# Starting products with three weight chunks at once, and copying a 128 MB table in 1 MB pieces beside the weight stream, in a two-block transformer kernel

## The chip, the cores and the metric

The kernel runs on one core of one Trainium2 chip. The metric is the device time of one execution in microseconds. Between runs of this kernel a difference of about 0.2% can be told from none.

## The reference, cut to what matters

Two transformer blocks are applied to 512 tokens of width 1024, all in float32. The first has a modulation (a product of a conditioning vector with a 1024 x 6144 matrix), RMS norms, neighbourhood attention, a gated recurrent mixer (HGRN2) and a feed-forward part (PEER) that gathers rows of two tables. The second block has two layers, each a mixer, a layer norm, a gated feed-forward part with a short convolution, and a second layer norm.

```python
h  = modulate(rms_norm(x, norm1), sh1, sc1) @ w_in      # q k v | hq zf zb i g; k v zf zb i of 256 context tokens too
x  = x + gt1 * (concat([na_x, hg_x]) @ w_out)
x  = x + gt2 * peer_ffn(modulate(rms_norm(x, norm2), sh2, sc2), peer_wq, peer_keys, peer_u, peer_v)
...                                                     # peer_ffn: for each token 128 rows of u and of v (16384 x 1024 each)
x  = rms_norm(x, norm_f)
for l in range(2):                                      # second block
    x = layer_norm(ALPHA * x + mixer(x), ln1_g[l], ln1_b[l])
    x = layer_norm(ALPHA * x + conv_ffn(x), ln2_g[l], ln2_b[l])
```

## The kernel before

All five engines run programs written out by hand, kept in step by semaphores; at 19 points (`barrier(eng, n)`) an engine drains itself (`eng.drain()`, line 161), counts up `phase` and waits until four engines have done so. With `passing` it counts up without waiting.

**Weights.** All weights come as one stream of chunks of 512 KB (128 partitions x 1024 numbers). `SECTIONS` gives their order: 16 chunks for the first part of the modulation (`mod1`), 4 each for q, k, v, hq, zf, zb, i, g, then `mod2` (24) and `mod3` (8), `out` (8), `wq` (16), and the second block's `rq`, `rk`, ..., `out_e`, `up0`, `down0`, `dq`, ..., `out_o`, `up1`, `down1`; `FIRST[name]` is a section's first chunk. SyncE (SP) loads chunk c into slot c % 4 of `RING` once chunk c - 4 has been used (line 366). VectorE splits each chunk of a product into a high part and a low part (`split_chunk`, lines 1289 and 1291). For most products three chunks are split ahead of need (`first_chunks`).

**Products.** One chunk gives 128 output features for all 512 tokens: for each of 8 input tiles k (128 features) `three_passes` issues high x high, high x low and low x high (lines 192 to 194), 24 matmuls of 512 columns in all. `tiles` runs the chunks of a section one after the other, with three PSUM banks in turn. After a norm, or where the mixer's output is new, the input tiles are themselves made one by one: VectorE scales a tile (line 1324), ScalarE applies gain and shift (973), VectorE splits it (1305, 1307) and counts up `x_split`. The first chunk of such a product waits for its tile before each three matmuls (`split(name, k)`). `follow` is the work that TensorE does for the next norm or, in `wq`, for the key scores behind each chunk. The `up` products are a loop of their own (`weights_up`) with four banks.

**The table.** The gathers of PEER read rows of one internal table `PEER_UV` (16384 x 2048) in which row n holds row n of u beside row n of v. The kernel makes it by copies from HBM to HBM: `copy_rows`, 32 copies of 1024 rows (4 MB) each, all issued by GpSimd (POOL): 9 before barrier 1, 15 between barriers 1 and 2 (from the ninth copy on each waits for the copy eight before it), and one at every fourth of the 32 attention tiles, between barriers 2 and 3. GpSimd waits for all of them before the first gather.

**Order of the work.** Norm of x and context; `mod1` on TensorE; splits of 8 x tiles and 8 context tiles; q, then barrier 1 for all engines but TensorE, which only passes it; k to g; barrier 2; 32 attention tiles, in each of which GpSimd makes a bias tile (line 402); barrier 3; the recurrent mixer in two directions with the `mod2` and `mod3` chunks placed in it (`modulate`, line 550), six of them at the start of each direction; barrier 6; `out`, norm, `wq`, PEER, norm; second block.

Of the kernel before, what the change touches and what calls it, by code (L numbers as in the profile page):

```python
# [26 lines left out]
D = 1024  # L27
# [27 lines left out]
EXP_AT = [24, 88] + [SLOTS * j + 56 for j in range(1, TT - 1)]  # L55
COPY_ROWS = 1024
COPIES = 2 * NKEYS * NKEYS // COPY_ROWS
COPIES_AHEAD = 8

# [7 lines left out]
for _name, _n in SECTIONS:  # L67
    FIRST[_name] = NCHUNK
    NCHUNK += _n


# [27 lines left out]
def build(nc, t):  # L99
    ctx = ExitStack()  # L100
    place = {}
    with ctx:
# [219 lines left out]
        def after(eng, s, key, n, per):  # L322
# [12 lines left out]
        pk_s, pk_sc, pk_top, pk_exp, pk_idx = (sem(f"pk_{k}") for k in ("s", "sc", "top", "exp", "idx"))  # L335
        uv_copied = [sem(f"peer_uv_copied{j}") for j in range(COPIES_AHEAD)]
        row_landed = [sem(f"row_landed{j}") for j in range(NROW)]
# [10 lines left out]
                                          "sum", "root")}  # L348

        nc_block = ctx.enter_context(nc.Block())  # L350


        @nc_block.sync
        def _(sp):
            sp.dma_start(XL[:], t["xl"]).then_inc(s_in, 16)
            sp.dma_start(PAR[:], t["par"]).then_inc(s_in, 16)
            sp.dma_start(XC[:], t["xc"]).then_inc(s_in, 16)
            sp.dma_start(IDN[:], t["ident"]).then_inc(s_in, 16)
            sp.dma_start(ONES[:], t["ones"]).then_inc(s_in, 16)
            for j in range(NSLOT):  # L360
                sp.dma_start(RING[:, j, :], t["wstream"][j]).then_inc(w_landed[j], 16)
            with sp.Fori(1, NCHUNK // NSLOT) as g:
                for j in range(NSLOT):

                    sp.wait_ge(chunk_used, g * NSLOT + (j - NSLOT + 1))
                    sp.dma_start(RING[:, j, :], t["wstream"][g * NSLOT + j]).then_inc(w_landed[j], 16)
            sp.wait_ge(phase, 4 * 19)
            sp.dma_start(t["out"], XL[:]).then_inc(s_out, 16)
            sp.wait_ge(s_out, 16)
# [3 lines left out]
        def _(pool):  # L373
            steps = Steps(pool, pool_step)
            pool.dma_start(BT, t["na_bias"]).then_inc(s_bt, 16)
            copies = iter(range(COPIES))

            def copy_rows(n):

                for i in itertools.islice(copies, n):  # L380
                    rows, x = slice(COPY_ROWS * (i // 2), COPY_ROWS * (i // 2 + 1)), i % 2
                    if i >= COPIES_AHEAD:
                        pool.wait_ge(uv_copied[i % COPIES_AHEAD], 16 * (i // COPIES_AHEAD))
                    pool.dma_start(PEER_UV[rows, D * x:D * x + D], t[("peer_u", "peer_v")[x]][rows]
                                   ).then_inc(uv_copied[i % COPIES_AHEAD], 16)

            pool.wait_ge(s_in, 80)
            copy_rows(9)
            barrier(pool, 1)
            copy_rows(15)  # L390
            barrier(pool, 2)
# [3 lines left out]
            for i in range(NA_HEADS * NCB):  # L395
                h, b = divmod(i, NCB)
                off = QB * b - KC0[b]
                if i >= 3:
                    pool.wait_ge(na["s"], i - 2)
                if i % 4 == 0:  # L400
                    copy_rows(1)
                pool.tensor_tensor(NBM[i % 3].rearrange("p (k j) -> p k j", k=NA_KH), BT[:, h, :, QB - off:QB - off + KB],
                                   par("na_mask")[:, KB * b:KB * b + KB].unsqueeze(1).to_broadcast([P, NA_KH, KB]),
                                   ALU.add).then_inc(na["bias"], 1)
# [29 lines left out]
            barrier(pool, 7)  # L434
            for j in range(COPIES_AHEAD):
                pool.wait_ge(uv_copied[j], 16 * (COPIES // COPIES_AHEAD))
            pool.wait_ge(chunk_used, FIRST["wq"] + 16)
# [27 lines left out]
        def _(pe):  # L465
# [11 lines left out]
            def tiles(c, n, xs, name, to, free, base=0, xs2=None, to2=None, follow=None):  # L477

                for i in range(n):
                    pe.wait_ge(w_split, nth_split(c + i) + 1)  # L480
# [6 lines left out]
                    for k in range(KT):  # L487
                        if b == 0:
                            split(name, k)
                        mm = three_passes(to(b), parts(c + i, k), tile(xs, k), pe, k == 0, k == KT - 1)  # L490
# [351 lines left out]
            def ffn(l):  # L842

                u, c0 = up[l], FIRST[f"up{l}"]
                with pe.Fori(0, 2 * FT // BLK) as g:
                    for j in range(BLK):
                        weights_up(pe, u, c0, g, j)
                for j in range(2 * FT % BLK):
                    weights_up(pe, u, c0, 2 * FT // BLK, j)
                after(pe, u, "act", 4 + FT, FT)  # L850
# [20 lines left out]
            def weights_up(pe, u, c0, g, j):  # L871
                pe.wait_ge(w_split, g * BLK + (nth_split(c0 + j) + 1))
                pe.wait_ge(u["evac"], g * BLK + (2 * FT * u["use"] + j + 1))
                for k in range(KT):
                    if j == 0:
                        split(("x3", "x5")[u["use"]], k)
                    mm = three_passes(bank(j % 4), parts(c0 + j, k), tile(XFS, k), pe, k == 0, k == KT - 1)
# [63 lines left out]
            passing(pe, 17)  # L941

            tiles(FIRST["out_o"], KT, MIXS, "mix3", main, ln[2], follow=mean(ln[2]))
            variance(ln[2])
# [974 lines left out]
```

## Time and profile before

| | us |
|---|---|
| median of 3 runs (lowest, highest) | 3895.64 (3894.32, 3897.06) |
| the profiled execution, its own time | 3882.41 |
| its span | 3880.6 |
| TensorE busy, share of the span | 3198.9, 82% |
| VectorE busy, share of the span | 2138.6, 55% |

The span is the time from the first to the last instruction that the profiler saw; all times "at" some microsecond count from its start. The profiled execution was 0.34% faster than the median of the timed runs, so its rows are used for differences, and a difference is then taken off the median.

### The profile page before, as it was taken

How to read it: one execution, taken by the hardware profiler on the slowest of the kernel's cores; microseconds unless marked ns; L12 is line 12 of the kernel's file. 1: busy time of each engine (PE TensorE's matmuls, PEld its weight loads, DVE VectorE, ACT ScalarE, POOL GpSimd, SP SyncE). 2: the span in 40 equal slices, each digit the busy share in tenths (PEclk: the TensorE clock that was granted, in tenths of full speed). 3: DMA queues.
4: the chain of work that ended last, by engine and by line, in shares of the span. 5: the costliest groups of instructions: out<-in, count | busy, mean ns of one | idle time of the engine just before them, and what ended most of it. 6: DMA issues, size and time to landing. Idle time of an engine off the chain costs nothing. (4 is left out here: it accounts for less than half of the span.)

```text
span 3880.6 us, 34820 instructions
## 1 busy us (share of the span) xinstructions
PE 3198.9 (82%) x12170; PEld 2142.1 (55%) x12170; DVE 2138.6 (55%) x3672; ACT 890.6 (23%) x2174; POOL 691.3 (18%) x655
## 2 busy tenths in 40 slices
PE   6499888788777777777777789778999899779998
PEld 6388677666222222322222267366887686458876
DVE  2122368656776774685444462346774434767753
ACT  2011333122222222222222220151220102312201
POOL 0000234101444343443343320000000000000000
PEclk6699888899999999999999999579999998889999
DMA  9999852125999999999999822001332230013322
GB/s 356 298 337 350 266 180 82 60 66 196 421 421 422 417 417 421 416 410 421 418 419 422 373 84 87 0 1 60 98 97 87 86 99 28 1 49 98 97 87 71
DMA packets 152752, 845.71 MB, mean 218 GB/s; under 512 B 13793, under 2 KB 14049, under 8 KB 86049
## 3 DMA queue, kind: packets, MB, share of 16 engines
q0 software_dynamic: 107968, 678.73, 44.8%
q1 hardware_dynamic: 44640, 165.12, 13.5%
q8 instruction: 84, 1.38, 0.1%
q14 instruction: 60, 0.48, 0.0%
HBM read 841.70 MB, written 136.31 MB: 252 GB/s over the span
## 5 line engine op out<-in xcount | busy, mean ns | idle before, releaser
L721 PE MATMUL PS<-AR,HC 128*128 128x512 f32 x1536 | 726.7, 618 | 249.0 <-ACT HC L1138 247.4
L192 PE MATMUL PS<-AR_r,RHI 128*128 128x512 f32 x1888 | 767.9, 407 | 182.9 <-DVE AR_r L1307 94.3
L194 PE MATMUL PS<-AR_r,RING_r 128*128 128x512 f32 x1888 | 746.7, 396 | 0.0
L1492 DVE SCALAR_TENSOR_TENSOR AR<-AR 128x1024 f32<-128x1024 f32 x384 | 470.2, 1225 | 359.7 <-DMA AR<-peer_uv,XC 356.9
L721 PEld LDWEIGHTS PS<-AR,HC 128*128 128x128 f32 x1536 | 283.5, 194 | 691.3 <-ACT HC L1138 393.2
L193 PE MATMUL PS<-AR_r,RHI 128*128 128x512 f32 x1504 | 594.8, 395 | 0.0
L445 POOL DMA_INDIRECT AR<-peer_uv,XC x384 | 398.7, 1038 | 739.8 <-PE PS L721 545.0
L192 PEld LDWEIGHTS PS<-AR_r,RHI 128*128 128x128 f32 x1888 | 361.8, 192 | 292.8 <-issue 89.7
L1289 DVE CAST RHI<-RING 128x1024 fp32r<-128x1024 f32 x256 | 178.6, 698 | 582.7 <-DMA RING<-in_wstream 519.3
L194 PEld LDWEIGHTS PS<-AR_r,RING_r 128*128 128x128 f32 x1888 | 362.2, 192 | 77.4
L193 PEld LDWEIGHTS PS<-AR_r,RHI 128*128 128x128 f32 x1504 | 288.6, 192 | 62.6 <-issue 6.0
L1291 DVE TENSOR_TENSOR RING_r<-RING,RHI 128x1024 fp32r<-128x1024 f32 x256 | 315.8, 1234 | 8.8
L721 PE MATMUL PS<-RHI_f,HC 128*128 128x512 f32 x512 | 240.0, 612 | 83.8 <-ACT HC L1138 82.4
L1129 ACT ACTIVATE XC<-XC 128x2 f32<-128x2 f32 x256 | 52.0, 203 | 924.7 <-DVE AR L1492 924.5
L1492 DVE SCALAR_TENSOR_TENSOR AR<-RHI_f,AR 128x1024 f32<-128x1024 f32 x128 | 156.6, 1225 | 122.9 <-DMA RHI_f<-peer_uv,XC 122.6
L721 PEld LDWEIGHTS PS<-RHI_f,HC 128*128 128x128 f32 x512 | 93.3, 192 | 230.2 <-ACT HC L1138 133.1
L1138 ACT ACTIVATE HC<-IDN,HC 128x128 f32<-128x128 f32 x512 | 173.7, 386 | 0.0
L445 POOL DMA_INDIRECT RHI_f<-peer_uv,XC x128 | 132.3, 1033 | 190.6 <-PE PS L721 186.8
L193 PE MATMUL PS<-HL_r,RHI 128*128 128x512 f32 x384 | 153.1, 399 | 0.0
L550 PE MATMUL PS<-CS,RING 128*128 128x2 f32 x768 | 129.2, 304 | 15.8 <-POOLq L161 10.6
L459 POOL DMA_DIRECT2D AR<-in_strips x1 | 0.7, 664 | 775.6 <-DVEq L161 775.6
L550 PEld LDWEIGHTS PS<-CS,RING 128*128 128x128 f32 x768 | 129.5, 267 | 16.8 <-POOLq L161 10.8
(314 smaller groups left out, 3677.8 us busy)
## 6 DMA issues: line engine op xcount, KB each, us to landing
RING<-in_wstream SPq DMA_DIRECT2D x304, 512.0 KB, 3.6
peer_uv<-in_peer_u POOLq DMA_DIRECT2D x16, 4096.0 KB, 80.6
peer_uv<-in_peer_v POOLq DMA_DIRECT2D x16, 4096.0 KB, 83.5
AR<-peer_uv,XC POOLq DMA_INDIRECT x384, 13.6
XL<-in_xl SPq DMA_DIRECT2D x1, 2048.0 KB, 9.9
RHI_f<-peer_uv,XC POOLq DMA_INDIRECT x128, 13.6
AR<-in_strips POOLq DMA_DIRECT2D x1, 2048.0 KB, 10.3
out_x<-XL SPq DMA_DIRECT2D x1, 2048.0 KB, 6.3
```

Of the source, the lines that this page charges most:

```text
L192: pe.matmul(out, sh, mh, start=start, stop=False)
L193: pe.matmul(out, sh, ml, start=False, stop=False)
L194: return pe.matmul(out, sl, mh, start=False, stop=stop)
L445: pool.indirect_dma_start(ROWS_UV[n % NROW], None, PEER_UV, bass.IndirectOffsetOnAxis(ap=IDX[:, n:n + 1], axis=0)).then_inc(row_landed[n % ...
L459: pool.dma_start(STRIP, t["strips"]).then_inc(s_strip, 16)
L550: mm = pe.matmul(bank(7, 2 * i, 2), part(RING, c + i, P * k, P), CS[:, 2 * k:2 * k + 2], start=(k == 0), stop=(k == KT - 1))
L721: mm = pe.matmul(bank(2 * (tt % 2) + x), DIAG[:, n % NDIAG, :], ROWS_UV[n % NROW][:, D + 512 * x:D + 512 * x + 512], start=(j == 0), stop= ...
L1129: act.activation(GA[:, n:n + 2], RAW[:, n:n + 2], ACT.Gelu).then_inc(gelu, 1)
L1138: act.activation(DIAG[:, (n + x) % NDIAG, :], IDN[:], ACT.Copy, scale=WEIGHT[:, n + x:n + x + 1]).then_inc(diag_ready, 1)
L1289: dve.tensor_copy(hi, x).then_inc(w_high, 1)
L1291: dve.tensor_tensor(lo, x, hi.bitcast(F32), ALU.subtract).then_inc(w_split, 1)
L1492: dve.scalar_tensor_tensor(JUNK[n % 2], ROWS_UV[n % NROW][:, 0:D], 1.0, HT[:, n // SLOTS, :], ALU.mult, ALU.mult, accum_out=RAW[:, n:n + 1 ...
```

## The change

The copies become 128 of 256 rows (1 MB). 96 of them are issued by SP, in the same queue as the weights: one after each weight chunk from the first of q to the last of `wq`, and two after every fourth chunk of `mod2` and `mod3`. The other 32 are issued by GpSimd, one before each bias tile of the attention, with a semaphore of their own. No copy waits for another one. GpSimd issues none before barriers 1 and 2. SP's loop is written out for the chunks up to `wq`.

In `tiles`, a section that begins at bank 0 takes its first three chunks together: TensorE waits until the third is split, and then does nine matmuls per input tile, three for each chunk, into three banks. This is so for q, `out`, `wq`, `rq`, `out_e`, `dq` and `out_o`, and `ffn` does the same by hand for `up0` and `up1`. The chunk counts go up only in the last input tile, and `follow(0)` comes right behind. Before `out_o` TensorE also waits for three of the roots, since banks 0 to 2 hold their sums.

```diff
-COPY_ROWS = 1024
+COPY_ROWS = 256
 COPIES = 2 * NKEYS * NKEYS // COPY_ROWS
-COPIES_AHEAD = 8
+COPIES_AFTER, _n = {}, 0
+for _c in range(FIRST["q"], FIRST["rq"]):
+    _more = 2 if FIRST["mod2"] <= _c < FIRST["out"] and _c % 4 == 0 else 1
+    COPIES_AFTER[_c] = range(_n, _n + _more)
+    _n += _more
+assert _n + NA_HEADS * NCB == COPIES
...
+        def copy_rows(eng, i, done):
+
+            rows, x = slice(COPY_ROWS * (i // 2), COPY_ROWS * (i // 2 + 1)), i % 2
+            eng.dma_start(PEER_UV[rows, D * x:D * x + D], t[("peer_u", "peer_v")[x]][rows]).then_inc(done, 16)
...
-            for j in range(NSLOT):
-                sp.dma_start(RING[:, j, :], t["wstream"][j]).then_inc(w_landed[j], 16)
-            with sp.Fori(1, NCHUNK // NSLOT) as g:
+            for c in range(FIRST["rq"]):
+                if c >= NSLOT:
+                    sp.wait_ge(chunk_used, c - NSLOT + 1)
+                sp.dma_start(RING[:, c % NSLOT, :], t["wstream"][c]).then_inc(w_landed[c % NSLOT], 16)
+                for i in COPIES_AFTER.get(c, ()):
+                    copy_rows(sp, i, uv_copied)
+            with sp.Fori(FIRST["rq"] // NSLOT, NCHUNK // NSLOT) as g:
...
-            pool.wait_ge(s_in, 80)
-            copy_rows(9)
             barrier(pool, 1)
-            copy_rows(15)
             barrier(pool, 2)
...
-                if i % 4 == 0:
-                    copy_rows(1)
+                copy_rows(pool, COPIES - 1 - i, uv_copied_late)
...
-                for i in range(n):
+                together = 3 if base == 0 else 0
+                if together:
+                    pe.wait_ge(w_split, nth_split(c + together - 1) + 1)
+                for k in range(KT if together else 0):
+                    split(name, k)
+                    for i in range(together):
+                        mm = three_passes(to(i), parts(c + i, k), tile(xs, k), pe, k == 0, k == KT - 1)
+                        if k == KT - 1:
+                            mm.then_inc(chunk_used, 1)
+                if together and follow is not None:
+                    follow(0)
+                for i in range(together, n):
...
+                pe.wait_ge(w_split, nth_split(c0 + 2) + 1)
+                pe.wait_ge(u["evac"], 2 * FT * l + 3)
+                for k in range(KT):
+                    split(("x3", "x5")[l], k)
+                    for j in range(3):
+                        mm = three_passes(bank(j), parts(c0 + j, k), tile(XFS, k), pe, k == 0, k == KT - 1)
+                        if k == KT - 1:
+                            mm.then_inc(chunk_used, 1)
+                weights_up(pe, u, c0, 0, 3)
                 with pe.Fori(0, 2 * FT // BLK) as g:
-                    for j in range(BLK):
+                    for j in range(4, 4 + BLK):
                         weights_up(pe, u, c0, g, j)
...
+            pe.wait_ge(df["root"], 3)
             tiles(FIRST["out_o"], KT, MIXS, "mix3", main, ln[2], follow=mean(ln[2]))
```

## Rows read from the trace of the kernel before

**Rows 1.** The page: the span in 40 slices of 97 us, two of its rows.
```profile
PE   6499888788777777777777789778999899779998
...
GB/s 356 298 337 350 266 180 82 60 66 196 421 421 422 417 417 421 416 410 421 418 419 422 373 84 87 0 1 60 98 97 87 86 99 28 1 49 98 97 87 71
```

**Rows 2.** Timeline about barrier 1: start us, us, instruction, idle before and what ended it.
```profile
105.35 0.43 DVE L1307 TENSOR_TENSOR HC_r<-HC,XC_r 128x256 fp32r<-128x256 f32 x1
165.30 0.69 DVE L1289 CAST RHI<-RING 128x1024 fp32r<-128x1024 f32 x1 [59.53 <-POOLq L161]
...
111.97 0.39 PE L194 MATMUL PS<-AR_r,RING_r 128*128 128x512 f32 x1
167.31 0.80 PE L192 MATMUL PS<-AR_r,RHI 128*128 128x512 f32 x1 [54.95 <-DVE RING_r L1291]
```

**Rows 3.** Timeline of POOL, 30 to 520 us, the rows behind its two long drains.
```profile
165.86 0.75 POOL L384 DMA_DIRECT2D peer_uv<-in_peer_v  x1 [126.21 <-POOLq L161]
...
407.75 0.55 POOL L392 DMA_DIRECT2D XC<-in_level_masks  x1 [116.22 <-POOLq L161]
```

**Rows 4.** Timeline: the last instruction ahead of barrier 2; PE and SP behind barrier 3.
```profile
395.04 0.60 ACT L1044 ACTIVATE AR<-PS 128x512 f32<-128x512 f32 x1 [4.84 <-PE PS L194]
...
528.84 20.64 PE L550 MATMUL PS<-CS,RING 128*128 128x2 f32 x96 [10.55 <-POOLq L161]
532.60 25.67 SPq L366 DMA_DIRECT2D RING<-in_wstream  x7
```

**Rows 5.** Stages: window, length, busy us (instructions) of PE, PEld, DVE, ACT, POOL, PEclk, DMA share, GB/s.
```profile
17.00:165.00 148.00, 81.48 (x360) 72.15 (x360) 31.90 (x59) 18.45 (x23) 6.43 (x9) 0.62 0.99 332
408.00:529.00 121.00, 108.37 (x577) 78.16 (x577) 51.55 (x129) 42.03 (x97) 32.85 (x43) 0.89 0.98 287
528.80:751.50 222.70, 180.73 (x1288) 175.52 (x1288) 163.88 (x209) 66.26 (x67) 86.21 (x60) 0.81 0.26 76
```

**Rows 6.** DMA issues (KB each, median us to landing); then landing of the first four chunks alone.
```profile
RING<-in_wstream SPq DMA_DIRECT2D x304, 512.0 KB, 3.6
...
DMA to landing us min/median/max: 14.3/15.4/17.7
```

**Rows 7.** Timeline of `mod1`: the matmuls of its last 12 chunks.
```profile
44.41 41.12 PE L550 MATMUL PS<-CS,RING 128*128 128x2 f32 x192 [3.08 <-DMA RING<-in_wstream]
```

**Rows 8.** POOL in one attention tile with a copy, and in one without.
```profile
443.78 0.77 POOL L384 DMA_DIRECT2D peer_uv<-in_peer_v  x1 [2.63 <-PE PS L601]
...
449.85 0.73 POOL L402 TENSOR_TENSOR HC<-AR,PAR 128x256 f32<-128x256 f32 x1 [2.41 <-PE PS L601]
```

**Rows 9.** PE alone by window: first chunk of `wq`, its next two; first of `up0`, of `up1`; q's three.
```profile
822.30:833.50 11.20, 10.07 (x24) 0.72 0.00 0
833.50:844.40 10.90, 10.90 (x49) 1.00 0.31 96
2688.50:2699.80 11.30, 9.10 (x25) 0.84 0.00 0
3475.60:3486.80 11.20, 9.59 (x24) 0.77 0.00 0
93.10:112.20 19.10, 19.02 (x72) 0.87 1.02 318
```

**Rows 10.** Timeline: neighbouring matmuls at the low clock; roots, last tile and next sum of `out_o`.
```profile
168.33 0.63 PE L194 MATMUL PS<-AR_r,RING_r 128*128 128x512 f32 x1
168.76 0.63 PE L192 MATMUL PS<-AR_r,RHI 128*128 128x512 f32 x1
...
3367.16 4.74 ACT L960 ACTIVATE HL<-PS,PAR 128x512 f32<-128x512 f32 x8
...
3409.93 0.80 PE L192 MATMUL PS<-AR_r,RHI 128*128 128x512 f32 x1 [3.59 <-DVE AR_r L1307]
...
3424.39 1.02 PE L531 MATMUL PS<-XL,ONES 128*128 128x512 f32 x2
```

**Rows 11.** Drains of POOL: ns min/median/max, first and last start in us.
```profile
L161 POOLq DRAIN  x19: 34/53/126390, 38.9 to 3486.0; - x19
```

More of the change, by code:

```diff
@@ L11 @@
-import itertools
 from contextlib import ExitStack
@@ L335, in build @@
         pk_s, pk_sc, pk_top, pk_exp, pk_idx = (sem(f"pk_{k}") for k in ("s", "sc", "top", "exp", "idx"))
-        uv_copied = [sem(f"peer_uv_copied{j}") for j in range(COPIES_AHEAD)]
+        uv_copied, uv_copied_late = sem("peer_uv_copied"), sem("peer_uv_copied_late")
         row_landed = [sem(f"row_landed{j}") for j in range(NROW)]
@@ L375, in _ @@
             pool.dma_start(BT, t["na_bias"]).then_inc(s_bt, 16)
[L376 to L385, printed above, removed]
-            pool.wait_ge(s_in, 80)
-            copy_rows(9)
             barrier(pool, 1)
-            copy_rows(15)
             barrier(pool, 2)
@@ L434, in _ @@
             barrier(pool, 7)
-            for j in range(COPIES_AHEAD):
-                pool.wait_ge(uv_copied[j], 16 * (COPIES // COPIES_AHEAD))
+            pool.wait_ge(uv_copied, 16 * (COPIES - NA_HEADS * NCB))
+            pool.wait_ge(uv_copied_late, 16 * NA_HEADS * NCB)
             pool.wait_ge(chunk_used, FIRST["wq"] + 16)
@@ L487, in tiles @@
                     for k in range(KT):
-                        if b == 0:
-                            split(name, k)
                         mm = three_passes(to(b), parts(c + i, k), tile(xs, k), pe, k == 0, k == KT - 1)
@@ L844, in ffn @@
                 u, c0 = up[l], FIRST[f"up{l}"]
+                pe.wait_ge(w_split, nth_split(c0 + 2) + 1)
[7 more added lines that the diff above has]
+                weights_up(pe, u, c0, 0, 3)
                 with pe.Fori(0, 2 * FT // BLK) as g:
-                    for j in range(BLK):
+                    for j in range(4, 4 + BLK):
                         weights_up(pe, u, c0, g, j)
-                for j in range(2 * FT % BLK):
-                    weights_up(pe, u, c0, 2 * FT // BLK, j)
                 after(pe, u, "act", 4 + FT, FT)
@@ L874, in weights_up @@
                 for k in range(KT):
-                    if j == 0:
-                        split(("x3", "x5")[u["use"]], k)
                     mm = three_passes(bank(j % 4), parts(c0 + j, k), tile(XFS, k), pe, k == 0, k == KT - 1)
```

## The prediction, made before the changed kernel was run

> **What bounds the kernel now.** I read the page first. TensorE is busy for 82% of the span, and the traffic shows two loaded stretches: the first 530 us, where the table is copied, and the gathers in the middle [rows 1]. The change touches the first stretch and the starts of nine products, so I looked for TensorE's idle time there. The list of waits has one wait of 55 us on TensorE, and the timeline about it shows what it is: VectorE ends its last context split at 105.8 us, then stands at barrier 1 for 59.5 us until POOL's drain is over, and TensorE runs out of split chunks at 112.2 and resumes at 167.3 [rows 2]. Behind its ninth copy POOL drained from 38.9 on for 126.39 us, where the median of its 19 drains is 53 ns [rows 3, 11]. Over that time the DMA engines were 99% busy [rows 5]. So a drain of POOL lasts until its copies are through, and whoever stands at that barrier pays for it. The same is seen twice more: barrier 2 falls at 407.75 although ScalarE's last eviction ended at 395.6 [rows 3, 4], and TensorE is released from barrier 3 after 10.55 us of waiting for POOL's queue [rows 4]. Elsewhere in q to g TensorE has work at its own pace, and the DMA is no bound.
>
> **The copies leave POOL ahead of barriers 1 and 2.** Barrier 1 then waits for VectorE, whose drain starts at 105.8. VectorE splits chunk 3 of q (0.69 + 1.23 us) by 108, while TensorE is busy till about 112, so the 54.95 us go. After the stall TensorE restarted at a granted 0.5 (1.2 GHz): matmuls are 0.427 us apart there [rows 10], and at full clock, 2.4 GHz, 10.9/48 = 0.227 [rows 9]. The slow part lasted 5.7 us, which is 5.7 x (1 - 0.227/0.427) = 2.7 us. Sum 57.7 us. Barrier 2: the eviction ends at 395.64 and ScalarE drains in under 1 us, so release is near 396.5 in place of 407.75: 11.2 us. Nothing else is late there: GpSimd's program up to barrier 2 is then empty. If TensorE keeps its clock over the shorter pause, up to 2 us more.
>
> **`mod1` without copies beside it.** Chunk 4 came late: TensorE stood 3.08 us before 44.41 [rows 7]. A chunk takes 3.6 us to land in the median [rows 6], and it was asked for when the first of the sixteen was used, three chunks of TensorE's time before need, so 3.1 us go. The other 12 chunks took 3.43 us each at the low clock. The six chunks after barrier 3, four of them already landed, took 20.64/6 = 3.44 each [rows 4]; so that pace is TensorE's own, and nothing is gained there.
>
> **What the copies cost in SP's queue.** No row shows a copy and a weight chunk in one queue. Below, a chunk passes a copy at no cost (0). Above, it waits for all of it. The gathers move 421 GB/s [rows 1], so a chunk (0.52 MB) is 1.25 us of transfer; the copies with weights beside them ran at 332 GB/s and the attention's at 287 [rows 5], 3.2 to 3.65 us for 1.05 MB; I take 3.5, and 4.75 for the pair. I take the upper case, since one queue issued in order is likeliest to be served in order. TensorE needs 24 x 0.227 = 5.45 us for a chunk, and half as much again where context tiles go along. So in q to g (32 pairs, 152 us of transfers, 230 of TensorE), `out` and `wq` the pair fits inside one chunk's work, and each load is asked for three chunks ahead. In the mixer 32 chunks and 40 copies want 40 + 140 = 180 us of 222.7 [rows 5]. Its tightest place is the opening burst of six: the fifth is asked for at 532.6 [rows 4] and lands at 536, its two copies run till 543, the sixth lands at 544.3 and is needed at 546. The cover is 1.7 us; a copy of 4.4 us would use it up, and from there every us more costs 2. I book nothing. The last copy is issued when `wq`'s twelfth chunk is used, over 20 us before the first gather at 934.6, so POOL's final waits cost nothing. What an SP wait holds back is only the next load, as before.
>
> The Trainium skill ("DMA: Bandwidth & Descriptors", section on queues, rings and completion order) says that a DMA engine takes descriptors of one ring in order and goes round between rings; by that rule a weight chunk that shared the engines with POOL's copies will now stand behind SP's, as my upper case has it. The trace of before has no copy in SP's queue that could show it.
>
> **Attention and barrier 3.** POOL issues 24 more DMAs of 0.77 us, 18.5 us in all. It stands 2.41 us in a tile without a copy and 2.63 in one with it, waiting for the scores of three tiles earlier [rows 8]; its bias tile is needed two tiles (6.3 us) later, so they are hidden, except in the first three tiles where it does not wait: 1 us lost. The bytes are the same 33.5 MB, offered at 1.05 MB per 3.14 us = 334 GB/s where 287 were served; so the queue is still the last to finish, about 120 us after barrier 2, and the wait of 10.55 us at barrier 3 stays. I book 0; at 332 GB/s the copies would end with the attention and 10 us would go; SP's leftovers from g (one or two copies) could cost 5.
>
> **Three chunks at once.** Behind a norm a tile comes every 1.67 us. `wq`'s first chunk took 11.2 us, the next two 10.9, together 22.0 [rows 9]. After the change all 72 matmuls lie in one dense row, since nine matmuls (2.0 us at full clock, 3.8 at half) outlast the tile's 1.67. With a half-clock start of h us the time is 16.3 + 0.47 h. From the clock of the first windows h = (1 - clock)/0.5 x length: 6.3 for `wq` (0.72), 3.6 for `up0` (0.84), 5.2 for `up1` (0.77) [rows 9]; `rq` and `dq` begin as `wq` does (clocks 0.73 and 0.72). Gains: 2.7, 2.9, 4.0, 2.7, 3.3, sum 15.6 us. In q, `out` and `out_e` tiles come every 1.06 us and the first chunk is dense already: 19.1 us for three [rows 9], against 16.3 + 0.47 x 4.9 = 18.6; the 0.5 us goes again to `follow(0)`, which now has to wait for its eviction and square. I book 0. `out_o`: a tile comes every 5.24 us. From the last one TensorE has 14.5 us to the end of the third chunk [rows 10]. After, it has nine matmuls, 3.8 us, and a low-clock tail of 0.8: 9.8 us gained; 12 if the clock is high by then, 8 if the low clock lasts longer. The waits added are met early: the third chunk is split before the first tile, the third root is out by 3367.16 + 3 x 4.74/8 = 3369 [rows 10], four us ahead of the first tile at 3373. The three slots come free together, 1.4 us before the end; the fourth chunk is there, the fifth lands and is split (3.6 + 1.9 us) 4.1 us after it, ahead of the 5.45 at which it is wanted. I take 1 us off for such edges.
>
> **Sum.** 57.7 + 11.2 + 3.1 - 1 + 15.6 + 9.8 - 1 = 95.4 us. 3882.4 - 95.4 = 3787.0 for the profiled execution; off the median of 3895.6 it is 3800.
>
> **Rivals.**
> (a) *The copies hold weights up somewhat.* A copy of 4.5 to 5.5 us instead of 3.5 leaves the mixer short: 40 x 5 + 40 = 240 against 222.7 and some us at each burst. 10 to 60 us lost, 3810 to 3860, 3830 as its middle. For it: 287 GB/s in the attention. Against it: 332 with weights between. 0.13.
> (b) *Slower than before.* The place is SP's queue. If transfers in it do not overlap, each pays its landing: a chunk 3.6, a copy 3.5 + 2.35 = 5.85. Then q to g needs 32 x 9.45 = 302 us of 230, the mixer 115 + 234 = 349 of 222.7, `out` and `wq` 24 x 9.45 = 227 of about 165: 260 us lost, 4060. It decides from a copy of 6.3 us mean, where 96 x 6.3 + 110 passes the 620 us of these stages by 95. Against it: at the start SP issued its inputs (3.6 MB) and four chunks in one go, and the chunks landed 14.3 to 17.7 us after their issue [rows 6], 5.7 MB in about 20 us, with no such cost in each. 0.04.
> The same page of the Trainium skill (section "Anatomy of one DMA") fits a transfer as 2.0 us + bytes/436e3; as an estimate that is 4.4 us for a copy, and if the fixed part did not overlap in a queue, it would be this rival.
> (c) *Barrier 3 opens with the attention*, and the clock stays up behind barrier 2: 12 us more, 3788. 0.15.
> (d) *The joint start gives nothing*, since the low clock lasts longer under it or the fifth chunk comes late: 25 us less gained, 3825. For it: three slots refilled at once. 0.08.
> (e) As summed, 0.60; its own range is 3790 to 3812.
>
> **Range and chances.** Cases (c), (e) and most of (a) and (d): 3782 to 3838. Only (b) ends slower. Faster by over 0.2% 0.95, within 0.2% 0.01, slower 0.04; 0.2% is about what a measurement of this kernel tells from no change.
>
> **What would show it.** No idle time of TensorE between chunks 2 and 3 of q; POOL drains under 1 us at barriers 1 and 2, and one of some 20 us at barrier 3; weight chunks from q to `wq` landing in 3.6 to 8 us with VectorE's waits for them covered; 72 matmuls in a row behind each norm, in about 19 us. Wrong would make it: TensorE waiting for splits in q to g or in the mixer's bursts, or POOL waiting for `uv_copied` before the gathers.

## The result, and the profile after

The changed kernel takes 3774.43 us (median of 4 runs: 3763.89, 3765.65, 3783.21, 3789.34). The kernel before took 3894.98 us (3888.78 to 3897.06) beside it. The ratio is 0.9696 [0.9654, 0.9737]: 120.6 us faster, where I had forecast 95 us faster, 3800 us, and a range from 3782 to 3838. The four runs lie on two levels some 20 us apart; the profiled execution (3763.89 us, span 3762.1) is of the faster one, and what separates the two levels is told below. So the 0.2% that I gave above as what can be told between runs is too little: the 43 timed runs of the kernel before lie from 3850.76 to 3897.06 us, 1.2% apart.

The page of the changed kernel: three of its rows over 40 slices of 94 us [rows 1 are their counterpart].
```profile
PE   6999887897777777777777789688999899789998
...
PEclk6998988899999999999999999789999998999999
...
GB/s 212 202 201 251 264 282 266 193 216 325 421 419 422 419 416 417 417 409 421 421 419 421 394 82 90 6 1 79 95 98 87 86 105 23 1 62 98 97 90 67
```
The copies' traffic is now spread: 193 to 282 GB/s through the first eight slices, where it had been 266 to 356 in the first five and 60 to 82 in the seventh to ninth.

The timeline of the changed kernel about barrier 1 and barrier 2 (VectorE, TensorE, ScalarE, GpSimd), against [rows 2 to 4].
```profile
103.67 0.69 DVE L1304 CAST RHI<-RING 128x1024 fp32r<-128x1024 f32 x1 [0.63 <-POOLq L167]
...
90.43 0.77 PE L198 MATMUL PS<-AR_r,RHI 128*128 128x512 f32 x1 [8.22 <-DVE HL_r L1322]
...
334.07 0.60 ACT L1059 ACTIVATE AR<-PS 128x512 f32<-128x512 f32 x1 [4.84 <-PE PS L200]
...
335.00 0.54 POOL L393 DMA_DIRECT2D XC<-in_level_masks  x1 [333.05 <-ACTq L167]
```
VectorE stands 0.63 us at barrier 1 in place of 59.53. From 90.43 to 120 us the view lists no idle time of TensorE; the 54.95 us are gone. GpSimd had nothing to do until ScalarE's last eviction, and barrier 2 opens 0.33 us after that eviction's end, at 335.00 where it was 407.75.

TensorE behind the attention, in the changed kernel, and below it the row of all drains of GpSimd, against [rows 4, 11].
```profile
446.40 1.96 PE L627 MATMUL PS<-HL,AR 128*64 128x128 f32 x16
465.61 17.23 PE L559 MATMUL PS<-CS,RING 128*128 128x2 f32 x80 [17.24 <-POOLq L167]
484.17 3.57 PE L559 MATMUL PS<-CS,RING 128*128 128x2 f32 x16 [1.33 <-DMA RING<-in_wstream]
...
L167 POOLq DRAIN  x19: 34/41/32770, 1.2 to 3370.3; - x19
```
The wait at barrier 3 did not stay at 10.55 us, it grew to 17.24. One drain of 32.77 us is left of the long ones. GpSimd's last copy, asked for at 432.73, landed at 464.2, and the drain ended at 465.6.

Windows of the changed kernel, columns as in rows 5: q to g; the attention; TensorE's wait at barrier 3; the mixer with `mod2` and `mod3`.
```profile
93.00:331.00 238.00, 233.91 (x1223) 200.68 (x1223) 65.28 (x83) 34.79 (x74) 0.00 (x0) 1.00 0.60 201
...
336.00:466.00 130.00, 110.97 (x578) 79.79 (x579) 66.79 (x129) 42.16 (x98) 43.53 (x66) 0.87 0.90 287
448.00:466.00 18.00, 0.76 (x6) 0.52 (x5) 0.46 (x2) 0.17 (x1) 0.34 (x1) 0.66 0.26 104
465.60:689.40 223.80, 178.50 (x1288) 172.82 (x1288) 164.20 (x208) 66.46 (x67) 86.14 (x60) 0.82 0.80 250
```
In q to g TensorE is busy for 98% at full clock with 201 GB/s beside it: nothing is starved. The mixer takes 223.8 us with all its copies, where it took 222.7 without.

DMA issues of the changed kernel (KB each, median us from issue to landing); the first row is of the whole span, the next two of q to g, then two of the attention, and the last three of the mixer (465.6 to 689.4).
```profile
RING<-in_wstream SPq DMA_DIRECT2D x304, 512.0 KB, 3.7
```
```profile
peer_uv<-in_peer_u SPq DMA_DIRECT2D x16, 1024.0 KB, 6.9
peer_uv<-in_peer_v SPq DMA_DIRECT2D x16, 1024.0 KB, 6.2
```
```profile
peer_uv<-in_peer_v POOLq DMA_DIRECT2D x16, 1024.0 KB, 22.1
peer_uv<-in_peer_u POOLq DMA_DIRECT2D x16, 1024.0 KB, 22.2
```
```profile
peer_uv<-in_peer_v SPq DMA_DIRECT2D x20, 1024.0 KB, 16.6
peer_uv<-in_peer_u SPq DMA_DIRECT2D x19, 1024.0 KB, 17.3
RING<-in_wstream SPq DMA_DIRECT2D x32, 512.0 KB, 14.3
```
The median of the whole span hides the mixer: there a weight chunk takes 14.3 us to land, four times the 3.7 us that it takes in q to g (and it takes 8.7 us in `out` and `wq`).

**Where the 118.5 us between the two spans come from.** Each line is the time at which the same instruction starts in the two traces.

| up to | before | after | gained so far | of it new | forecast |
|---|---|---|---|---|---|
| barrier 2 | 407.75 | 335.00 | 72.7 | 72.7 | 72.0 |
| barrier 3 | 528.84 | 465.61 | 63.2 | -9.5 | -1 |
| end of PEER | 2259.2 | 2196.3 | 62.9 | -0.3 | 2.7 |
| start of retention | 2423.3 | 2355.6 | 67.7 | 4.8 | 2.9 |
| end of retention | 2483.9 | 2390.5 | 93.4 | **25.7** | 0 |
| `up0` | 2699.2 | 2604.2 | 95.0 | 1.6 | 0 |
| end of its feed-forward | 3073.4 | 2975.1 | 98.3 | 3.3 | 4.0 |
| `dq` | 3144.8 | 3043.9 | 100.9 | 2.6 | 2.7 |
| behind differential attention | 3355.8 | 3251.5 | 104.3 | 3.4 | 0 |
| end of `out_o` | 3460.0 | 3344.3 | 115.7 | 11.4 | 9.8 |
| last instructions | 3871.7 | 3753.1 | 118.6 | 2.9 | 3.3 |

The -0.3 up to PEER's end is 2.2 gained in `wq` and 2.5 lost before it, most of it in the mixer. The table shows at once what I had missed: 25.7 us come from the retention stage of the second block (behind barrier 10), in which the change edits nothing, and barrier 3 gives 9.5 us back.

The windows ahead of and in the retention stage, first of the kernel before, then of the changed one.
```profile
2421.00:2424.00 3.00, 0.81 (x3) 0.45 (x3) 0.00 (x0) 2.07 (x4) 0.00 (x0) 1.00 0.55 153
2424.00:2482.00 58.00, 57.31 (x99) 25.38 (x98) 7.87 (x16) 2.39 (x4) 0.00 (x0) 0.53 0.00 1
```
```profile
2353.00:2356.00 3.00, 0.81 (x3) 0.29 (x2) 0.00 (x0) 2.06 (x4) 0.00 (x0) 1.00 0.45 117
2356.00:2410.00 54.00, 38.12 (x112) 17.83 (x110) 25.63 (x30) 8.61 (x13) 0.00 (x0) 0.90 0.01 4
```
The two rows of the three microseconds ahead are the same to the hundredth for TensorE. Then the granted clock falls to its lower level (1.2 GHz) in the kernel before, not in the pause but 2 to 3 us after TensorE has resumed, and in the changed kernel it stays at the upper one (2.4 GHz) for as long as the stage's own work lasts (the 0.90 holds a pause at its end). What TensorE did just ahead is one pause: it waited 2.19 us at barrier 10 for ScalarE, in both kernels. So the traces alone say where 25 us come from, and not why.

### The profile page after: what moved, and what is told of

It is laid out like the page before. It is cut to its first block and busy times, and to the rows that moved or that the text cites. A ratio compares the mean times of both kernels' runs of the same rounds, so it can differ in the third digit from the quotient of the medians.

```text
span 3762.1 us, 34565 instructions
## 1 busy us (share of the span) xinstructions
PE 3153.5 (84%) x12170; PEld 2129.0 (57%) x12170; DVE 2151.2 (57%) x3672; ACT 889.1 (24%) x2174; POOL 687.7 (18%) x655
```

## The experiments

Every kernel was timed beside the kernel before on its own chip; that one's medians were 3880.86, 3881.66, 3884.72 and 3879.04 us in the four sets of runs. "After" is the changed kernel.

**The two halves apart.** `copies_only` is the kernel before with the copies as the change has them, and the old starts of products. `joint_only` has the starts, and the copies as before.

> The kernel before with the copies moved (1 MB, SP's queue and the attention), its products started as before. Theory: the two traces stand 61.2 us apart at barrier 6, before any joint start but q's has acted, so this kernel gains about 61 us: 3834 against 3895, and in its trace barrier 2 falls near 335, barrier 3 near 465. The retention stage of the second block, 25 us shorter in the trace of the changed kernel, holds no edit; if the clock granted there is chance, this kernel has it either way: 3834 or 3811. Rival: the retention stage is short because the copies have left POOL: then always 3811.

Measured: 3813.01 us (3809.07 to 3817.94), ratio 0.9828 [0.9775, 0.9880]. Against the trace of before: 72.5 us gained at barrier 2, 64.5 at barrier 3 (TensorE waits 17.20 us there), and 64.5 at the end: nothing won or lost behind barrier 3. The median lies on the rival's 3811, but by chance: the 3834 of the theory counts from 3895, and on this chip the kernel before took 3880.86, so that 61 us less is 3820. The retention stage of the profiled run (3817.94) ran at the low clock, against the rival.

> The kernel before with the joint starts alone, its 4 MB copies on POOL as they were. Theory: wq 2.2, rq 2.9, up0 3.3, dq 2.8, out_o 11.6, up1 2.9 us as between the two traces: 26 us, 3869, stalls at barriers 1 to 3 as before. By chance of the clock in the retention stage 20 to 25 us less. Rival: the joint starts bring the retention stage's full clock, since rq starts it: then always near 3845.

Measured: 3848.33 us (median of 10; three near 3820, seven from 3845 to 3855), ratio 0.9912 [0.9879, 0.9945]. The trace is of a run of 3824.34: 34.8 us gained up to `up0`, 25.5 of them in the retention stage; `up0` 3.3, `dq` 2.7, `out_o` 11.5, `up1` 2.7. So the starts alone are worth some 30 us by the slower level, where 26 were expected (3.6 us more came in differential attention, see below), and the means of the two levels are 29 us apart. The rival's "always" fails: by their times seven of the ten runs don't have the stage's full clock.

**Is it the drain, or where the copies are?** `before_undrained` leaves all 4 MB copies on GpSimd and only takes its drain away, at barriers 1 to 3:
```diff
+        def undrained(eng, n):
+
+            eng.nop().then_inc(phase, 1)
+            eng.wait_ge(phase, 4 * n)
...
-            barrier(pool, 1)
+            undrained(pool, 1)
```


> The kernel before, in which POOL counts itself in at barriers 1 to 3 without draining; nothing else is changed, copies of 4 MB on POOL's queue. Theory: the drain, not the traffic, held barriers 1 to 3, so 55 + 2.7 (barrier 1), 11 (barrier 2) and 10.5 us (barrier 3) go, about 79 us: 3816. Rival: it was the traffic of 4 MB copies that would starve the weight chunks if TensorE went on; then chunks land later than TensorE needs them in q to g and less than 50 us are gained.

Measured: 3802.04 us (3773.93 to 3812.97), ratio 0.9795 [0.9723, 0.9867]. TensorE at barrier 3, and the DMA of 93 to 450 us, in that kernel:
```profile
447.61 18.61 PE L555 MATMUL PS<-CS,RING 128*128 128x2 f32 x96 [0.43 <-DVEq L161]
```
```profile
peer_uv<-in_peer_v POOLq DMA_DIRECT2D x12, 4096.0 KB, 111.6
peer_uv<-in_peer_u POOLq DMA_DIRECT2D x11, 4096.0 KB, 115.5
RING<-in_wstream SPq DMA_DIRECT2D x33, 512.0 KB, 8.8
```
The median is 79 us below before's on that chip, which is what was expected (3816 counts from 3895). Barrier 2 falls 70.8 us earlier than before, and barrier 3 opens at 447.6, 81.2 us earlier than before and 18 us earlier than after. Weight chunks take 8.8 us to land beside the 4 MB copies in place of 3.7, and TensorE still isn't starved (216.0 of 217 us busy from 93 to 310). Three changed instructions, then, are worth no less than moving all the copies (the medians, 3802 and 3813, lie within each other's intervals; by the traces it is 81.2 against 64.5 us at barrier 3): the cost was the drain, and the copies' place was only a way around it. The landings say the same of the kernel before: its three long drains end at 165.3, 407.2 and 528.8 us, and the last copy then outstanding landed at 164.8, 406.5 and 528.4.

**The changed kernel once more** (`after_again`, on the chip of the three above).

> The changed kernel once more, unchanged. Its four times lay at 3764, 3766, 3783 and 3789. Theory: the two levels are the retention stage at the full clock or at half of it; so the profile shows its TensorE clock near 1.0 over the 40 us behind barrier 10 with a span near 3762, or near 0.5 there with a span of 3782 to 3788. Rival: the levels come from elsewhere (copies, gathers), and the stage is at full clock in both.

Measured: 3787.77 us (3758.05; 3786.20 to 3789.40 the other four), ratio 0.9768 [0.9716, 0.9820]. On this chip the median is 93 us below before's; of nine runs of the changed kernel in all, three lie near 3762 and six near 3787. The profiled run is the fastest one (3758.05), with the full clock in the retention stage, so it could only confirm half of the theory; a slower run is first profiled below. Its wait at barrier 3 is 13.6 us.

**Barrier 3 without the drain.** `after_undrained3` is the changed kernel with the edit above at barrier 3 alone, behind a wait for the masks that GpSimd makes.

> The changed kernel, with one thing different: at barrier 3 GpSimd (POOL) waits for the masks and counts itself in, without a drain, so the barrier opens while its 1 MB table copies are still moving. Theory (the 17.2 us that TensorE waits at barrier 3 in the profile after is the drain of GpSimd behind its last copies, and nothing there needs them): the stage behind barrier 3 starts about 16 us earlier and all of it reaches the end: about 3770 us where the changed kernel takes 3786, about 3746 where the retention stage has its full clock (3762 to 3766 in the changed kernel). Rival (the copies' last traffic holds the first weight chunks of the GLU stage up): the wait moves to the weight chunks, gain under 8 us.

Measured: 3743.20, and 3776.16, 3777.31, 3779.91 us; ratio 0.9715 [0.9642, 0.9787]. Barrier 3 opens at 451.0, 14.6 us earlier, and the stage behind keeps that. At the faster level the time is what was expected (3746); at the slower one it is 7 us above the expected 3770. The profiled run (3776.16) is of the slower level, and shows what the levels are. The windows ahead of and in its retention stage:
```profile
2337.00:2340.00 3.00, 2.05 (x5) 1.04 (x6) 0.00 (x0) 0.86 (x2) 0.00 (x0) 0.99 0.51 164
2340.00:2398.00 58.00, 57.31 (x94) 25.39 (x93) 7.86 (x16) 2.39 (x4) 0.00 (x0) 0.50 0.00 0
```
This kernel has the change's starts, and has the low clock in the stage all the same: the stage's clock is not a matter of which kernel runs but of which run it is. The clock is at 0.50 from 2340, two us after TensorE resumed, and the stage loses 28.7 us against after's trace (63.8 us in place of 34.9); in the kernel before it lost 25.7.

**Filling the pause.** `after_filled` puts four matmuls whose result nobody uses into the 2.19 us ahead of barrier 10:
```diff
+            pe.wait_ge(free, 24)
+            for n in range(4):
+                pe.matmul(bank(4 + n % 2), IDN[:], XL[:, n, :], start=True, stop=True)
             barrier(pe, 10)
```


> The changed kernel, with four float32 matmuls of unused result put in front of barrier 10, ahead of the retention stage, where TensorE otherwise pauses some 2.3 us. Theory (whether the retention stage gets the full clock is decided by what TensorE does just before it, and the four matmuls fill that pause): full clock in the stage in every run, all runs near 3765 us plus the 1 to 2 us of the matmuls, none near 3786. Rival (the two levels of the runs have another origin than that pause): the two levels of 3762 and 3786 us stay, in much the same shares.

Measured: 3763.18, 3758.06, 3756.99, 3755.24 us; ratio 0.9689 [0.9634, 0.9744]. No run near 3786. `before_filled` has the same edit on the kernel before, and nothing else:

> The kernel before, and nothing of the change in it, with the four float32 matmuls of unused result ahead of barrier 10. Theory (the clock of the retention stage is settled by TensorE's pause just ahead of it, whatever the rest of the kernel does): full clock in that stage in every run, no run above 3875 us, the profiled span near 3856 us; so the 25 us of that stage are no part of what the change is worth. Rival (three-chunk starts are needed for the full clock there): the stage stays at half clock and the median stays near 3882 us, or 1 to 2 us above.

Measured: 3855.12 us (3851.08 to 3855.82, 5 runs), ratio 0.9933 [0.9911, 0.9954]; before beside it ran from 3870.02 to 3890.55. The windows of `before_filled` ahead of and in the stage:
```profile
2424.00:2427.00 3.00, 2.92 (x8) 1.42 (x8) 0.62 (x1) 0.00 (x0) 0.00 (x0) 1.00 0.00 0
2427.00:2479.00 52.00, 35.86 (x106) 16.71 (x104) 25.26 (x30) 8.61 (x13) 0.00 (x0) 0.88 0.00 0
```
The pause is gone and the clock stays up, in the unchanged kernel too, and the stage ends 24.6 us earlier than in before's trace (it starts 1 us later, for the four matmuls). Its level is that of the fastest runs of before, six of 39 (3850.76 to 3856.58 us). So the rival of that run falls: joint starts are not needed. All five kernels with the four matmuls agree with themselves within 3 to 8 us in 21 runs; the runs of one kernel without them spread over 20 to 41 us in each set (`copies_only`, 9, and the first set of before, 8, aside). With the stage's clock equal on both sides, the change is worth 3855.12 - 3757.53 = 97.6 us (the medians of before beside the two were 3884.72 and 3881.66, so some 3 us of it may be the chips'). The two traces give 88.7 us, since the profiled run of `after_filled` is its slowest (3763.18), so the value is uncertain by some 10 us; the 95 us of the forecast lie inside.

**Less traffic in the attention.** `after_half_late` is the changed kernel with 16 of the attention's 32 copies moved to SP's queue in q to g (two behind every even chunk).

> The changed kernel with half of the 32 table copies of the attention stage moved to the SP queue in the stages ahead of it (two after every even weight chunk of the first products), the other 16 on GpSimd at every other tile. Theory (barrier 3 opens late because of what GpSimd has outstanding at its drain, and the first stages have transfer time to spare): barrier 3 near 450 us on the span's scale, where it stands at 466, and 12 to 16 us less at the end. Rival (the first stages have none to spare: weight chunks land late): barrier 2 opens 5 us or more later than the 335 of the changed kernel and takes the gain back.

Measured: 3751.59, and 3770.84 to 3782.19 us; ratio 0.9741 [0.9684, 0.9797]. GpSimd's drain ends at 445.0, before the attention's own end at 456.4: the wait is gone. But TensorE's first matmul of q came at 97.6 (90.4 after), and barrier 2 8.6 us later; 12.3 us of gain are left at the end, by traces of the faster level, the lower end of the 12 to 16 expected. Both theories hold in part.

**All copies left on GpSimd, with both good edits.** `joint_undrained` is `before_undrained` and the change's starts together; `joint_both` adds the four matmuls, and `after_both` is the changed kernel with no drain at barrier 3 and the four matmuls.

> The kernel before with two things different: the products that follow a norm begin with three weight chunks at once (the change's first half), and GpSimd counts itself in at barriers 1, 2 and 3 without a drain; the table copies stay on GpSimd's queue in pieces of 4 MB as they were. Theory (the drain alone was the cost; pacing the copies by the weight chunks is worth nothing on top of that): the sum of the two halves measured apart, 81 to 88 us for the drains and about 34 us for the joint starts, so about 3760 to 3765 us without the full clock in retention, about 3740 with it: 20 us under the changed kernel of the same level. Rival (4 MB copies beside the three-chunk start hold the weight chunks up, which the pacing avoids): 3785 us or more, level with the changed kernel.

Measured: 3751.36, and 3774.95 to 3783.98 us; ratio 0.9746 [0.9690, 0.9802]: 11 us above the expected time at the faster level, 10 to 20 at the slower one. The first theory is wrong by about half of a gain of 20 us, and the rival's 3785 wasn't reached either; why, the next two show.

> The kernel before with its copies left on GpSimd in pieces of 4 MB, no drain at barriers 1, 2 and 3, the three-chunk starts and the four matmuls ahead of barrier 10. Theory (the pacing of the copies in 1 MB pieces is worth nothing once the drains are gone): within 6 us of the changed kernel with both edits, 3740 to 3750 us in every run.

> The changed kernel with both edits that worked: barrier 3 without GpSimd's drain and the four matmuls ahead of barrier 10. If the two add up: 3742 us in every run (3757.5 with the four matmuls alone, less the 15 us that barrier 3 opened earlier). If the full clock in the four runs of that kernel was luck, runs near 3770 us are back.

Measured: `joint_both` 3754.30 us (3749.58 to 3757.35), ratio 0.9671 [0.9643, 0.9700]; `after_both` 3745.15 us (3742.50 to 3747.19), ratio 0.9648 [0.9620, 0.9675]. `after_both` is 3 us above the expected 3742, with no run near 3770. For `joint_both` the expected 3740 to 3750 us and the difference of at most 6 us are missed: the medians are 9 us apart, and the two kernels' runs don't overlap. By their traces `joint_both` is 12.9 us late at barrier 2, 14.7 at barrier 3 and 8.1 at the end (6 of `after_both`'s lead are lost in the mixer, below). TensorE in q of `joint_both`:
```profile
94.44 0.76 PE L197 MATMUL PS<-AR_r,RHI 128*128 128x512 f32 x1 [8.07 <-DVE HL_r L1330]
123.66 0.47 PE L197 MATMUL PS<-AR_r,RHI 128*128 128x512 f32 x1 [4.42 <-DVE RING_r L1314]
```
`after_both` begins q at 90.33 and has no second wait. With three slots of the ring given back at once, the next chunks must land soon. The first of them, asked for at 112.6, took 8.8 us beside the 4 MB copies; in `after_both` it found SP's queue empty and took 3.7. That makes 4.42 us of stall, and q had begun 4.1 us later; the remaining 4 us were not traced in full. So pacing the copies does pay, but mainly since the starts are joint: at barrier 2 it is worth 2 us against `before_undrained` and 12.9 here.

**The burst behind barrier 3.** `after_both` gains 83.2 us at barrier 3 and has 77.3 left in the mixer. TensorE and SP's queue there:
```profile
455.08 3.58 PE L565 MATMUL PS<-CS,RING 128*128 128x2 f32 x16 [0.17 <-DMA RING<-in_wstream]
468.73 3.57 PE L565 MATMUL PS<-CS,RING 128*128 128x2 f32 x16 [10.07 <-DMA RING<-in_wstream]
...
454.94 2.98 SPq L379 DMA_DIRECT2D RING<-in_wstream  x1
457.96 3.41 SPq L364 DMA_DIRECT2D peer_uv<-in_peer_v  x1
461.41 3.72 SPq L379 DMA_DIRECT2D RING<-in_wstream  x1
```
The sixth chunk comes 10.07 us late. It was asked for at 449.38 and landed at 468.68, 19.3 us later. Ahead of it in SP's queue stood the fifth chunk's two copies, which landed at 460.5 and 464.4 while GpSimd's last copy was still moving (till 467.7). Besides, an issue that costs SP 0.33 us elsewhere costs it 3 to 4 here; but these issues come after that of the late chunk, and so did not delay it. `after_spread` drops the eight copies of this burst and puts them behind every third chunk of `out` and `wq`:

> The changed kernel with both edits (barrier 3 without GpSimd's drain, four matmuls ahead of barrier 10) and one more: no copies behind the first six chunks of mod2; their eight go behind every third chunk of out and wq, which then have two. Theory (with barrier 3 open early, TensorE waited 10.1 us for a weight chunk in the burst of six that follows it, because SP's copies of that burst met GpSimd's last ones): that wait goes, 6 to 8 us less, 3737 to 3740 us in every run, with out and wq no longer. Rival (it is GpSimd's copies alone that hold the chunk up, or out and wq grow with two copies behind a chunk): no faster than 3745 us.

Measured: 3756.76 us (3754.98 to 3758.18), ratio 0.9704 [0.9647, 0.9761]. The mixer is 6.8 us faster, as expected, and `out` to the end of PEER 12.4 us slower, the rest of the span 4.3 more: 9.1 us lost at the end. The rival has it: `out` and `wq` grow. The windows of `out` and the landings of the weight chunks from there to 860, first of `after_both`, then of `after_spread`:
```profile
682.80:745.80 63.00, 52.61 (x208) 39.97 (x209) 33.98 (x45) 7.97 (x12) 0.00 (x0) 0.93 0.65 204
...
RING<-in_wstream SPq DMA_DIRECT2D x24, 512.0 KB, 7.7
```
```profile
675.20:744.70 69.50, 52.85 (x208) 39.77 (x208) 33.91 (x45) 7.96 (x12) 0.00 (x0) 0.89 0.76 245
...
RING<-in_wstream SPq DMA_DIRECT2D x24, 512.0 KB, 14.1
```
The same 208 matmuls take 69.5 us in place of 63, with weight chunks that land in 14.1 us in place of 7.7. `after_both` stays the best of all kernels here, 29 us under the changed kernel's median of 3774.43, by medians of two chips.

## Why the prediction was wrong

**The step that failed is one that was not in the sum: the clock of the retention stage, booked at nothing because nothing is edited there.** It is worth 25.7 us between the two traces (25.5 in `joint_only`, 28.7 from `after_undrained3` to after), a run has it or has not, and a pause of 2.19 us of TensorE ahead of the stage is what leaves it open: the prediction has no term for it. The profiled run of before did not have it, three of nine of after did. Two of the four runs behind 3774.43 had it, by their times. By the slower level alone (3783, 3789) the time lies inside the forecast's range, though below its own range of 3790 to 3812. The forecast for the profiled execution was 3787.0, and it took 3763.89: the 25.7 us are more than the whole difference. Of the medians they explain only half, since only two of the four runs have them. The slower two (3786.3 in the mean) still lie 13.7 us below the forecast of 3800, because I had carried over the 13 us between before's median and its profiled execution as if they were fixed. They were not: 28 of the 35 later runs of before lie below the lowest of the four that I started from (3888.78), and on the chip of `after_again` the slower level of the changed kernel is 93 us under before's median, near the forecast's 95.

What decides in a single run whether the clock falls over an identical pause stays open; that the pause is necessary for the fall is shown by 21 runs without it, none of which is at the slower level. Whether the starts raise the share of runs that have it is open too: by their times 9 of 32 runs of the kernels with joint starts and without the four matmuls, against 6 of 39 of before, are of the faster level, which may be chance.

**Barriers 1 and 2:** 72.7 us against 72.0 forecast. The reading of the two long drains was right, and `before_undrained` shows it with the copies left where they were (70.8).

**Barrier 3 was mis-sized.** I booked 0 and kept 5 us as a bound for SP's leftovers; it cost 9.5. The wait is 17.24 in place of 10.55, and the attention itself took 2.9 us longer at a clock of 0.87. The argument "same bytes, so the same end" left out that the last copies of g came on top: three of SP's landed only from 336.7 to 354.7, and SP's queue moved 2.61 MB from 336 us on, 9 us at the 287 GB/s of the window. In all it is 37 MB in 130 us, where 35 had been moved in 121 [rows 5]. More than that, I left the wait as given. It was the same drain as at the other two, and the cheapest 15 us in the kernel.

**SP's queue (rivals a and b):** almost no loss (2.5 us ahead of `wq`, most of it in the mixer). Transfers of one queue do overlap, which ends rival (b): the 32 pairs fit in 238 us, where copies of 6.2 to 6.9 us and chunks of 3.7, paying one after the other, would need 32 x 10 = 320. That a chunk waits for the copies ahead of it, the upper case, is what the mixer shows. Two issues of SP, the first in the microsecond from 473, the second in that from 476:
```profile
peer_uv<-in_peer_v SPq DMA_DIRECT2D x1, 1024.0 KB, 15.9
```
```profile
RING<-in_wstream SPq DMA_DIRECT2D x1, 512.0 KB, 13.5
```
The copy, asked for at 473.00, landed at 488.9, and the chunk, asked for at 476.04, at 489.6. So it goes for the four chunks asked for from 472.63 to 482.87: each lands within a microsecond behind the copy ahead of it. Here the trace agrees with the rule that I cited from the Trainium skill's page "DMA: Bandwidth & Descriptors" (section "Queues, rings and completion order"), that a ring's descriptors are taken in order. My estimate of 4.4 us for a copy used that page's fit (section "Anatomy of one DMA"), which it gives for DMAs of GpSimd; the quickest copy in SP's queue in q to g took 5.7 us. The sign that I had named, chunks landing in 3.6 to 8 us up to `wq`, failed in the mixer (14.3 us) and in `out` and `wq` (8.7), and it cost next to nothing, since a chunk is asked for three chunks ahead. The tightest place was named rightly, and its size was not: behind barrier 3 the two copies ahead of the sixth chunk took 10.6 us in place of 7.0, so the cover of 1.7 us was used up and TensorE waited 1.33 us in after; once barrier 3 opened early, it waited 10.07.

**Joint starts:** `wq` 2.2 (forecast 2.7), `rq` with its neighbours 4.8 (2.9), `up0` 3.3 (4.0), `dq` 2.6 (2.7), `up1` 2.9 (3.3): 15.8 against 15.6. Windows of the changed kernel for `wq`, `up0`, `up1`, against [rows 9]:
```profile
761.50:780.90 19.40, 19.23 (x72) 15.64 (x73) 12.16 (x22) 5.10 (x8) 0.00 (x0) 0.84 0.01 2
2593.60:2613.00 19.40, 19.39 (x78) 15.90 (x79) 12.01 (x21) 6.24 (x8) 0.00 (x0) 0.90 0.06 13
3359.90:3379.30 19.40, 19.36 (x74) 15.81 (x75) 12.02 (x21) 5.43 (x7) 0.00 (x0) 0.86 0.03 5
```
`wq` has its 72 matmuls in 19.4 us, where I had 16.3 + 0.47 x 6.3 = 19.3; the other two windows already hold some of the next chunk's. `out_o` gave 11.4, the case that I had put beside 9.8 ("12 if the clock is high by then"); the last tile and the next sum in the changed kernel, against [rows 10]:
```profile
3305.80 0.50 PE L198 MATMUL PS<-AR_r,RHI 128*128 128x512 f32 x1 [1.37 <-DVE AR_r L1322]
...
3308.56 1.12 PE L540 MATMUL PS<-XL,ONES 128*128 128x512 f32 x2 [0.39 <-DVE XL L1697]
```
2.76 us from the last tile to the next sum: the clock was up.

**Differential attention:** 3.4 us with no edit in it, and it is the clock again. The same 35 us of this stage in before and in after (columns as in rows 5):
```profile
3231.00:3266.00 35.00, 35.00 (x84) 19.34 (x83) 12.56 (x40) 9.74 (x35) 0.00 (x0) 0.51 0.00 0
```
```profile
3129.00:3164.00 35.00, 35.00 (x95) 19.59 (x94) 12.66 (x40) 10.66 (x35) 0.00 (x0) 0.61 0.00 1
```
The low level lasts 34.1 us in before and 27.3 in after, and 6.8 us at half the clock cost 3.4. `copies_only` has before's clock (0.51) and no gain there; `before_undrained`, `before_filled`, `joint_only` and all other kernels have after's and the 3 us. It doesn't go with the retention stage's clock, which is low in `before_undrained` and high in `joint_only`. What lets the clock rise sooner stays open.

## What to carry to other kernels

Look at what a barrier does for the engine that issues DMAs: a drain behind copies that nobody at the barrier needs is worth its whole wait, and counting in without the drain (with a wait for what is really needed) is cheaper than moving the copies. Before a gain is put down to an edit, compare the granted clock stage by stage; a stage that can run at either level makes any comparison of a few runs uncertain by its whole difference, and a few matmuls in the pause ahead of it may settle it, in the old kernel as well as in the new one. Refilling several buffers at once needs quick transfers at that moment: two edits that are each harmless can cost 9 us together. And look at landings stage by stage: a median over the span (3.7 us here) can hide a stage with four times as much.

## What the runs showed of the hardware that I had not expected

- Behind the same pause of 2.19 us the granted clock fell to 0.5 in one run and stayed at 1.00 in another, and the stage behind kept what it got: 60.6 us for the stage at the low level, 34.9 at the high one. The fall came 2 to 3 us after TensorE had resumed, not in the pause.
- One core moved 347 GB/s through its DMA engines for 357 us with 4 MB copies outstanding on GpSimd's queue and weight loads on SP's, and the loads still landed in 8.8 us.
- In SP's queue a load of 512 KB that took 3.7 us to land by itself took 14.3 us behind copies of 1 MB: it landed just behind the copy issued before it.
- The time that SP spends in issuing a DMA is no constant: 0.33 us as a rule, 3 to 5 us for four issues in the burst behind barrier 3 of `after_both`.
